# Values products of the sample attention: from 128x32 tiles per sequence and group to one 128x64 tile per sequence

## What is computed

```python
# per sequence b, token t, group g, head p of the group
o_c = softmax(q.kc - slope*dist) @ vc            # 32 compressed blocks
o_s = softmax(q.k  - slope*dist | selected) @ v  # 2048 cached tokens (16 of 33 blocks) + 8 new
o_w = softmax(q.kw - slope*dist | window) @ vw   # 512 window tokens + 8 new
o   = gate_c * o_c + gate_s * o_s + gate_w * o_w
```

## Time and profile before

| | us |
|---|---|
| median of 3 runs | 909.55 (905.48 to 910.02) |
| the profiled execution | 906.55 |
| its span | 904.7 |
| TensorE busy | 826.2 (91%) |
| VectorE busy | 418.0 (46%) |
| ScalarE busy | 335.7 (37%) |
| GpSimd busy | 135.0 (15%) |

### The profile page before, as it was taken

The page is one execution under the profiler, slowest core; times in us unless marked ns, Lnnn a source line. Parts: engine busy times, 40 slices in busy tenths (PEclk is TensorE's granted clock), DMA queues, the critical chain, the costliest instruction groups (busy, mean ns, idle before and its releaser), DMA issues.

```text
span 904.7 us, 18157 instructions
## 1 busy us (share of the span) xinstructions
PE 826.2 (91%) x7775; PEld 752.2 (83%) x7775; DVE 418.0 (46%) x782; ACT 335.7 (37%) x626; POOL 135.0 (15%) x160
## 2 busy tenths in 40 slices
PE   5999998997888867785999999999999999999995
PEld 4999977775555645465999999999999999999995
DVE  5435646664555475565327433344233433243432
ACT  6511155552566565463225431133212331043311
POOL 0001101100785345530220000000000000000120
PEclk9999999998899889896999999999999999999998
DMA  8912628842461206526221122222221122222002
GB/s 299 323 72 95 192 70 248 259 168 93 134 206 36 83 1 233 190 79 178 94 93 50 48 89 93 93 93 93 93 86 41 59 93 93 94 93 93 1 1 105
DMA packets 48794, 103.03 MB, mean 114 GB/s; under 512 B 7499, under 2 KB 19167, under 8 KB 46430
## 3 DMA queue, kind: packets, MB, share of 16 engines
q1 hardware_dynamic: 41821, 68.61, 23.1%
q0 software_dynamic: 6912, 33.56, 10.9%
HBM read 97.75 MB, written 8.53 MB: 117 GB/s over the span
## 4 chain that ended last, share of the span: by engine, by line
PE 52%; DVE 1%; ACT 0%; DVEq 0%; issue 0%
PE banks L2003 51%; PE banks L2044 0%; DVE y L1993 0%; PE banks L2070 0%; DVE wl L1923 0%; PE banks L2060 0%; ACT wh L1867 0%; DVE hT L1936 0%; DVE hT L1961 0%; DVE xl L1940 0%; ACT low L1881 0%; DVE xl L1929 0%; ACT xh L1883 0%; DVEq L1816 0%; ACT small L1911 0%
## 5 line engine op out<-in xcount | busy, mean ns | idle before, releaser
L2003 PE MATMUL banks<-xh,wh 128*128 128x288 f32 x640 | 138.3, 298 | 4.3 <-DVE xl L1929 3.9
L2003 PE MATMUL banks<-xl,wh 128*128 128x288 f32 x640 | 138.1, 297 | 0.0
L2003 PE MATMUL banks<-xh,wl 128*128 128x288 f32 x640 | 137.7, 297 | 0.0
L1867 ACT ACTIVATE wh<-low 128x1024 fp32r<-128x1024 f32 x72 | 75.0, 1050 | 103.1 <-PE banks L2003 102.9
L2003 PE MATMUL banks<-ah,wh 128*128 128x288 f32 x512 | 110.2, 297 | 0.0
L2003 PE MATMUL banks<-al,wh 128*128 128x288 f32 x512 | 109.6, 296 | 0.0
L2003 PE MATMUL banks<-ah,wl 128*128 128x288 f32 x512 | 109.6, 296 | 0.0
L2003 PEld LDWEIGHTS banks<-xh,wh 128*128 128x128 f32 x640 | 104.0, 190 | 5.0 <-DVE wl L1923 4.2
L2003 PEld LDWEIGHTS banks<-xl,wh 128*128 128x128 f32 x640 | 104.1, 190 | 0.0
L2003 PEld LDWEIGHTS banks<-xh,wl 128*128 128x128 f32 x640 | 104.0, 190 | 0.0
L1961 DVE TENSOR_TENSOR hT<-banks,hT 128x288 f32<-128x288 f32 x64 | 26.3, 453 | 138.9 <-PE banks L2003 138.9
(11 more groups left out here) (340 smaller groups left out, 1372.3 us busy)
## 6 DMA issues: line engine op xcount, KB each, us to landing
low<-in_w_up SPq DMA_DIRECT2D x8, 2048.0 KB, 8.2
low<-in_w_down SPq DMA_DIRECT2D x8, 2048.0 KB, 7.7
zone<-in_cmp_w SPq DMA_DIRECT2D x16, 256.0 KB
o_swin<-in_state_win SPq DMA_DIRECT2D x8, 504.0 KB
px<-in_x_prompt SPq DMA_DIRECT2D x4, 512.0 KB, 5.3
u_raw<-in_w_in SPq DMA_DIRECT2D x1, 2048.0 KB, 10.0
q_raw<-in_w_in SPq DMA_DIRECT2D x1, 2048.0 KB, 10.4
low<-in_state_win SPq DMA_DIRECT2D x4, 512.0 KB
```

Source lines behind the costliest of these rows:

```text
L1867: act.activation(wcols(m.wh, i), raw_cols(i), ACT.Copy).then_inc(wh_ready, 1)
L2003: last = pe.matmul(out(i, hf), w[wi], half(x[:, k, :], hf), start=first and part == 0, stop=end and part == 2)
```

## The change

The values products lose the split by group. A product now takes all 64 probability columns of a sequence (both groups) as the stationary operand and the value columns of both groups (2 x 64) as the moving one; two such tiles stand side by side, one per sequence, without an explicit tile position. A step has 8 products in place of 16; half of each result (rows of one group, values of the other) is computed and not used. The small parts have 6 products in place of 12, and their order changes: for each sequence the compressed part first, then the two branches of new tokens. A branch now takes 128 columns of `pb[4]` in place of 64. The merge reads 128 columns of each branch in place of 64 columns read twice. Scores and everything else stay.

```diff
@@ merge (DVE)
-                both = lambda r: pb[4][:, HD * r:HD * r + HD].unsqueeze(1).broadcast_to([P, NKV, HD])
-                o_both = m.o_sb.rearrange("p (g d) -> p g d", g=NKV)
-                dve.tensor_scalar(o_both, both(0), ssum(n)[:, 0:1], None, ALU.mult).then_inc(o_step, 1)
+                dve.tensor_scalar(m.o_sb, pb[4][:, 0:P], ssum(n)[:, 0:1], None, ALU.mult).then_inc(o_step, 1)
                 for k, f in enumerate((ssum(n)[:, 1:2], m.grow[:, 3 * n:3 * n + 1])):
                     dve.wait_ge(o_step, n * O_STEPS + k + 1)
-                    dve.scalar_tensor_tensor(out=o_both, in0=both(k + 1), scalar=f, in1=o_both, op0=ALU.mult,
-                                             op1=ALU.add)\
+                    dve.scalar_tensor_tensor(out=m.o_sb, in0=pb[4][:, P * (k + 1):P * (k + 2)], scalar=f,
+                                             in1=m.o_sb, op0=ALU.mult, op1=ALU.add)\
@@ values (TensorE)
-                def out(e, g, r):
-                    return pb[4][rows_of(e, g), HD * r:HD * r + HD]
-
-                def probs(v, at, e, g):
-                    return v[:, at + 64 * e + 32 * g:at + 64 * e + 32 * g + 32]
-
+                out = lambda e, r: pb[4][64 * e:64 * e + 64, P * r:P * r + P]
                 for mm in range(QUAD if i < X else 0):
-                    for e, g in tiles:
-
-                        last = pe.matmul(out(e, g, int(ORDER[i] == 4)), probs(m.spT[i % 3], P * mm, e, g),
-                                         m.slot[2 * (n % 2) + e][:, ORDER[i], mm, P * g + HD:P * g + P],
-                                         start=(i == 0 and mm == 0), stop=False, skip_group_check=True,
-                                         tile_position=(0, 64 * e + 32 * g))
+                    for e in range(2):
+
+                        last = pe.matmul(out(e, int(ORDER[i] == 4)).rearrange("p (g d) -> p g d", g=NKV),
+                                         m.spT[i % 3][:, P * mm + 64 * e:P * mm + 64 * e + 64],
+                                         m.slot[2 * (n % 2) + e][:, ORDER[i], mm, :]
+                                         .rearrange("p (g k) -> p g k", g=NKV)[:, :, HD:2 * HD],
+                                         start=(i == 0 and mm == 0), stop=False, skip_group_check=True)
                 if i == X:
-                    for br in range(2):
-                        for e, g in tiles:
-                            pe.matmul(out(e, g, br), probs(m.spX[0:NS, :], P * br, e, g),
-                                      values_at(m, PTILES, br, NS)[:, HD * g:HD * g + HD], start=False, stop=False,
-                                      skip_group_check=True, tile_position=(0, 64 * e + 32 * g))
-                    for e, g in tiles:
-                        last = pe.matmul(out(e, g, 2), probs(m.spX[0:NBLK, :], 2 * P, e, g),
-                                         m.vc[:, 2 * n + e, HD * g:HD * g + HD], start=False, stop=True,
-                                         skip_group_check=True, tile_position=(0, 64 * e + 32 * g))
+                    for e in range(2):
+                        pe.matmul(out(e, 2), m.spX[0:NBLK, 2 * P + 64 * e:2 * P + 64 * e + 64], m.vc[:, 2 * n + e, :],
+                                  start=False, stop=False, skip_group_check=True)
+                        for br in range(2):
+                            last = pe.matmul(out(e, br), m.spX[0:NS, P * br + 64 * e:P * br + 64 * e + 64],
+                                             values_at(m, PTILES, br, NS), start=False, stop=(br == 1),
+                                             skip_group_check=True)
                 last.then_inc(v_done, 1)
```

## The result

| | before | after |
|---|---|---|
| median of ten runs on one chip (us) | 907.29 (903.63 to 910.02) | 911.55 (908.21 to 915.40) |
| ratio, 95% interval | 1 | 1.0052 (1.0032 to 1.0072) |
| the same kernel in a later comparison | 1 | 1.0030 (1.0008 to 1.0052) |
| span of the profiled execution (us) | 904.7 | 907.9 |
| first values product to first MLP product | 343.75 to 420.58: 76.8 | 346.33 to 424.24: 77.9 |

The change makes the kernel slower, by 4.3 us between the medians (4.7 by the ratio; 3.7 by the mean of the two ratios, 1.0041). The forecast was 2.2 us the other way. That the value itself, 911.55, lies in the forecast's range of 901.5 to 915 is luck as much as insight: the forecast started from 909.55, the median of three runs, and ten runs of the kernel before give 907.29.

A forecast was written before the change was run, and what follows sets the result against it. TensorE's MLP products were taken to bound the kernel, the change moving only their start. First and second pair -3.0, third and fourth with the stall +0.8, sum -2.2 us: median 907.3 from 909.55, range 901.5 to 915.

The forecast's parts named there:

- First and second pair, under the gathers: First two rounds of values products, beside the page gathers: fewer records win 1 and 2 us, -3.0 (-6 to +4).
- the time goes by the record: First two pairs' values: bursts and late signals follow the record count, so a stretch losing 88 records gets shorter.
- ACT's packing of the gather's first slot: Second pair: limits the win, packed at 379.98; TensorE could turn it near 380.65 instead of 382.01, 1.35 us to win.
- nothing to win under the gathers: Rival, first two pairs: late signals come with the traffic, not the records; +0.8 us, 910.4; chance 0.18.
- the last step: A pair's last group (new keys, compressed blocks): 0.60 us becomes 1.5, +0.9 a pair (+0.2 to +1.45).
- The group: Values products, 8 wide in place of 16: 0.59 us becomes 1.02, +0.43 a group.
- The third round: Third pair's values, on the path: they end at 404.9 in place of 402.97, +1.9 us.
- The stall: Fourth pair's fifth group: 3.87 us idle by "issue", read as an instruction fetch, goes; -4.0 us with the restart.
- The request that the prediction put near 405: TensorE asks for its next instruction block near 405, behind w_out's load in the DMA engines, and runs dry two blocks after the last.
- Third and fourth together: Third and fourth pair's values, on the path, with the stall's removal included: +0.8 us.
- the rival with 924: Rival: the two column sides do not overlap, a group takes 1.88 us; +15 in sum, 924; chance 0.10.
- The rule of the Trainium skill's: Values groups: about 60 cycles of overhead per matmul would make the change cost 0.07 us a group; the prediction rejected it.

The follow-up runs named there:

- late_wide: The changed kernel with slots' products wide in the third and fourth pair alone, as before in the first two; 909.35 us against 906.07 for the kernel before, ratio 1.0050.

## Why the prediction was wrong

**The step that failed** is "First and second pair, under the gathers: -3.0 us". It was read from two true facts: TensorE's records come in bursts beside the gathers, and the second pair's values end late. Both facts held in before. Two things built on them failed.

The first is that the time goes by the record, so that fewer records end the values sooner. In the two profiles taken first it looked so: the merge begins 10.7 us after the second round's values in place of 13.6. But over the fifteen profiles with gathers the two rounds' merges begin 21.9 to 29.1 us after their values, summed, with wide groups, and 22.5 to 26.8 with narrow ones. The second is that the next pair would gain by an earlier end. The prediction found the limit itself, ACT's packing of the gather's first slot, took it at 379.98 and granted 1.35 us behind it, plus 1.3 of late signals. The runs show that the slot is packed 10.2 to 11.2 us after the values' start in both profiles of either kernel (8.9 to 12.2 over all fifteen), and that late signals stay with fewer records (after has its own, 1.81 us and more) and go with the gathers: without them there are none.

Found in place of -3.0: +0.6 by the rounds' sums, +1.0 with 3 either way by timing. The rival "nothing to win under the gathers" said just this and was given 0.18; its reason against ("the fourth pair has more traffic and none") was weak, since the fourth pair's traffic is the load of w_out and no gather.

**Mis-sized: the last step**, 1.87 us where 1.5 was taken, inside its bounds (0.80 to 2.05). Nothing overlapped, as the upper bound had it; "neighbours share a side" was a reason for that end and not for the middle.

**What held.** The group, 1.02. The third round, forecast +1.9, is +2.3: the forecast and the last step's 0.37. The stall went, as the count of blocks had it, and a kernel that only adds instructions loses it too and is 4 us faster. The request that the prediction put near 405 is record 8191, near 405.9. The Trainium skill ("Runtime: NRT & Kernel Launch", section "Instruction fetch mechanics") calls such fetches mostly hidden; here the measurement decides, since this one left TensorE idle for 3.7 to 4.5 us beside the load of w_out. The fourth round is 1.3 us shorter (16.1 to 14.9; 1.0 in the second profiles, 16.0 to 15.0), 1.1 forecast. Third and fourth together: +1.0 (24.5 to 25.5), forecast +0.8. The two sides overlap, so the rival with 924 is out. The rule of the Trainium skill's "TensorEngine Tiling (Array Packing)", section "Instruction Overhead", by which a group would, as an estimate, cost 0.07 more, is out as well: it cost 0.43.

**The sum** by profiles is +0.6 and +1.0, or +1.6 us; the timings say +3.7, with some 1.4 either way. The 2.1 between them are more than the timings' error, though not more than it and the scatter of the rounds together, and no run assigns them. So by this sum more than half of the measured loss has no place in the profiles (the second pair of profiles alone gives +2.8). In the same direction, late_wide and the narrow kernels with the new last step stand 0.0082 apart by timing (1.0050 against a mean of 0.9968, 7.4 us) and 2.7 to 4.0 us apart by the third and fourth rounds of their profiles. So the wide groups may cost more in the late rounds, in executions that were not profiled, than the profiled ones show. This stays open.

**A version that beats both**: narrow groups with the wide last step, 0.9954, 0.9966 and 0.9984 in three comparisons, about 3 us faster than before. In the profiles the gain stands in the fourth round, 12.9 to 13.0 us against 16.0 and 16.1: it is the stall, gone because the stage ends 45 records short of the place. The last step by itself costs 1.3 a pair, or 0.35 by turns. Any later edit of the code ahead of that place can bring the stall back. By turns the profile was the shortest of all with gathers (899.0), but its first values product also came 3.1 us sooner than in before (340.69), behind shared code, and the timing, 0.9981, does not bear a gain of that size out.

## What to carry to other kernels

Half the instructions with twice the columns is no gain where narrow tiles on four sides already overlap: 0.59 us became 1.02. Before time is credited to a stretch beside heavy DMA, ask what starts the next stretch: here it was a transfer, and an end 2.9 us earlier brought the next start no nearer. Take more than one profile of such a stretch: the first pair showed the earlier end, and the others did not bear it out. And when a change moves the number of instructions, time a version that moves that number alone: here it was worth 4 us, as much as the whole effect under study.

## What the hardware showed that was not expected

- The stall is tied to a record's number: TensorE stood idle for 3.68 to 4.45 us behind 8447 records of the trace in four runs, one of them with other code at that place, and 192 records put in much earlier took it away (0.9955). The packet of the instruction queue that ends it starts 4.7 to 7.5 us after record 8191 there, and 0.7 us after it ahead of w_out's load.
- Six products of 64 stationary columns take 1.87 us with the side changing after every third and three changes of height, and 0.95 with the side changing each time and one. Of 64 rows, four by turns take as long as two on one side (0.59 and 0.58).
- With the gathers the first two rounds of before take 14.5 us more (52.3 against 37.8 without them), though ACT and DVE are busy for as long in both, 13.4 to 13.9 and 15 to 16 us a round. Beside them the clock falls from 1.00 to 0.93 and 0.81, and signals come late; what each of these costs was not separated.
- Products of ones in the gap ahead of the MLP hold the granted clock at 1.00 there (0.75 without them), and it falls all the same with the MLP's first product, for 3.5 us.
